# Feed-forward stages of a two-block transformer: gate and up products with the tokens stationary and 512 weight columns moving

## The reference

```python
def rms_norm(x, g):
    xf = x.astype(jnp.float32)
    y = xf * lax.rsqrt(jnp.mean(xf * xf, axis=-1, keepdims=True) + NORM_EPS)
    return (y * g.astype(jnp.float32)).astype(x.dtype)

def swiglu_ffn(h, w_in, w_out):
    gate, up = jnp.split(h @ w_in, 2, axis=-1)
    return (jax.nn.silu(gate) * up) @ w_out

x = x + FFN_RES_WEIGHT * swiglu_ffn(rms_norm(x, ffn1_norm_g[l]), ffn1_w_in[l], ffn1_w_out[l])
```

## Time and profile before

| quantity | value |
|---|---|
| median of 3 runs | 2745.47 us (2745.07 to 2746.79) |
| the profiled execution | 2742.86 us |
| its span, first to last instruction | 2740.9 us |
| mean granted TensorE clock | 0.973 of full speed |
| PE busy | 2630.0 us, 18787 matmul records |
| DVE busy | 1700.7 us |
| ACT busy | 1028.4 us |
| weights cast by ACT in feed-forward steps (L1150) | 132, 1915 ns each |
| low parts by DVE there (L1407) | 132, 2290 ns each |

### The profile page before, as it was taken

The page is one execution under the profiler, slowest core; times in us unless marked ns, Lnnn a source line. Parts: engine busy times, 40 slices in busy tenths (PEclk is TensorE's granted clock), DMA queues, the critical chain, the costliest instruction groups (busy, mean ns, idle before and its releaser), DMA issues. The chain is left out here.

```text
span 2740.9 us, 44687 instructions
## 1 busy us (share of the span) xinstructions
PE 2630.0 (96%) x18787; PEld 2324.0 (85%) x18787; DVE 1700.7 (62%) x2283; ACT 1028.4 (38%) x1275; POOL 99.2 (4%) x179
## 2 busy tenths in 40 slices
PE   8999989999989999989999999999999999989999
PEld 7999888989989999779899954355799899737999
DVE  6887655768768877656678822553455455354555
ACT  4335302444343354204443321643333333264333
POOL 2110000001101100000001000000000000000000
PEclk9999989999999999989999999889999999999999
DMA  8775201647766764004557752100355555210452
GB/s 277 261 260 185 93 1 47 200 140 244 261 216 223 264 224 154 16 1 138 171 174 258 260 193 77 46 1 31 127 183 183 199 184 185 78 62 31 140 183 93
DMA packets 279510, 415.63 MB, mean 152 GB/s; under 512 B 10105, under 2 KB 235721, under 8 KB 277698
## 3 DMA queue, kind: packets, MB, share of 16 engines
q1 hardware_dynamic: 260332, 348.16, 38.5%
q0 software_dynamic: 18128, 64.20, 6.8%
q10 hardware_dynamic: 902, 1.15, 0.1%
HBM read 399.82 MB, written 13.65 MB: 151 GB/s over the span
## 5 line engine op out<-in xcount | busy, mean ns | idle before, releaser
L614 PE MATMUL ps<-h_high,w_high 128*128 128x256 f32 x1984 | 567.9, 286 | 17.5 <-DVE w_low L1407 10.5
L616 PE MATMUL ps<-h_high,w_low 128*128 128x256 f32 x2016 | 572.3, 284 | 0.0
L614 PEld LDWEIGHTS ps<-h_high,w_high 128*128 128x128 f32 x1984 | 382.8, 193 | 20.3 <-DVE w_low L1407 11.4
L616 PEld LDWEIGHTS ps<-h_high,w_low 128*128 128x128 f32 x2016 | 389.0, 193 | 0.0
L1407 DVE TENSOR_TENSOR w_low<-ring,w_high 128x2048 fp32r<-128x2048 f32 x132 | 302.3, 2290 | 138.5 <-ACT w_high L1150 138.2
L615 PE MATMUL ps<-h_low,w_high 128*128 128x256 f32 x1312 | 373.4, 285 | 0.0
L2797 DVE TENSOR_TENSOR w_low<-ring,w_high 128x2048 fp32r<-128x2048 f32 x96 | 220.0, 2292 | 240.6 <-ACT w_high L2581 240.4
L1150 ACT ACTIVATE w_high<-ring 128x2048 fp32r<-128x2048 f32 x132 | 252.3, 1915 | 266.7 <-DMA ring<-in_ffn_w_in 147.9
L2581 ACT ACTIVATE w_high<-ring 128x2048 fp32r<-128x2048 f32 x96 | 183.8, 1916 | 331.2 <-PE ps L2260 304.1
L615 PEld LDWEIGHTS ps<-h_low,w_high 128*128 128x128 f32 x1312 | 254.0, 194 | 0.0
L1428 DVE SCALAR_TENSOR_TENSOR mod_acc<-wmod,cond,mod_acc 128x512 f32<-128x512 f32 x336 | 230.8, 748 | 0.0
(11 more groups left out here) (426 smaller groups left out, 5395.0 us busy)
## 6 DMA issues: line engine op xcount, KB each, us to landing
ring<-in_w_mlp SPq DMA_DIRECT2D x96, 1024.0 KB, 5.5
ring<-in_ffn_w_in SPq DMA_DIRECT2D x88, 1024.0 KB, 8.8
wmod<-in_w_mod POOLq DMA_DIRECT2D x96, 512.0 KB, 6.3
ring<-in_ffn_w_out SPq DMA_DIRECT2D x44, 1024.0 KB, 5.1
ring<-in_w_mix_in SPq DMA_DIRECT2D x26, 1024.0 KB, 5.5
ring<-in_xattn_w_kv SPq DMA_DIRECT2D x16, 1024.0 KB, 5.3
mod_scratch<-mod_acc POOLq DMA_DIRECT2D x24, 512.0 KB, 5.5
ring<-mod_scratch SPq DMA_DIRECT2D x12, 1024.0 KB, 6.8
```

Source lines behind the costliest of these rows:

```text
L614: mm(dst, w_hi, x_hi, start=start, stop=False, **more)
L616: return mm(dst, w_lo, x_hi, start=False, stop=stop, **more)
```

## The change

In all four stages the gate and up products are turned round. 128 tokens of x times the gain (`g_high`, `g_low`) are stationary, and the moving operand is 256 gate columns and 256 up columns of the weights in one access pattern, 512 wide. A step does the first 128 tokens (`half` 0), then the other 128, each into a bank of its own that holds gate and up side by side. For this the two high parts must lie at one stride, so their buffers are laid out in one tensor `span`, two pairs of gate and up, and the down high part has one buffer alone (the storage of `h_high`). The three float32 factors are the same.

The root of the norm is now a number per partition (`root_col`), made by sums on PE with one column; silu takes it as a scale, and the product with up multiplies by it. So the normalised copies for these stages go, and with them `first_apart`, `first_scaled` and two of the three `norm` calls.

The activation now has tokens on partitions. Four PE transposes (`turn`) bring it back, into a PSUM bank of its step; ACT casts the high part from there (`cast`) and DVE subtracts (`act_lower`). `turn(i + 1)` stands in the middle of `down(i)`.

```diff
+            def half_products(b, t, k, last=False):
+                out = ps[4 + 2 * b + t].rearrange("p (r n) -> p r n", r=2)
+                toks, cols, s = slice(t * P, (t + 1) * P), slice(k * BLK, (k + 1) * BLK), tiles.slot(0, b)
+                hi, lo = gate_up_high[b][:, :, cols], w_low[:, s:s + 2, cols]
+                mm(out, g_high[:, k, toks], hi, start=(k == 0), stop=False)
+                mm(out, g_high[:, k, toks], lo, start=False, stop=False)
+                if not last:
+                    return mm(out, g_low[:, k, toks], hi, start=False, stop=(k == KD - 1))
+                for r in range(2):
+                    mm(out[:, r, :], g_low[:, k, toks], hi[:, r, :], start=False, stop=(r == 1)
+                       ).then_inc(w_used[tiles.slot(r, b)].sem, 1)
...
+            def turn(i, b):
+                pe.wait_ge(*tiles.act(i, 2))
+                for t in range(2):
+                    for m in range(2):
+                        at = b * 512 + t * BLK + m * P
+                        last = nc.tensor.transpose(ps[4 + 2 * b][:, m * T + t * P:m * T + (t + 1) * P],
+                                                   act_tok[:, at:at + P], ident)
+                last.then_inc(act_turned.sem, 1)
...
             with pe.Fori(1, FFN_STEPS // 2) as j:
-                gate_up(j * 2 + 1, 1, j * 6 + 2, 2, True)
-                down(j * 2, 0, j * 6 + 4, 1)
-                gate_up(j * 2 + 2, 0, j * 6 + 5, 2, True)
-                down(j * 2 + 1, 1, j * 6 + 7, 1)
+            with pe.Fori(1, FFN_STEPS // 2 - 1) as j:
+                gate_up(1, j * 6 + 2)
+                down(j * 2, 0, j * 6 + 4, lambda: turn(j * 2 + 1, 1))
+                gate_up(0, j * 6 + 5)
+                down(j * 2 + 1, 1, j * 6 + 7, lambda: turn(j * 2 + 2, 0))
...
             with act.Fori(1, FFN_STEPS // 2) as j:
-                silu(j * 2, 0, j, True)
-                w_high_of(0, 1, j, 2, (0, 0, j))
-                w_high_of(1, 1, j, 0, (1, 0, j))
-                w_high_of(2, 0, j, 1, (2, 1, j - 1))
-                silu(j * 2 + 1, 1, j, True)
-                w_high_of(0, 0, j + 1, 2, (0, 1, j))
-                w_high_of(1, 0, j + 1, 0, (1, 1, j))
-                w_high_of(2, 1, j, 1, (2, 0, j))
+            with act.Fori(1, FFN_STEPS // 2 - 1) as j:
+                silu(j * 2, 0, j)
+                w_high_part(tiles, 2, 0, j, DOWN_HIGH, (2, 1, j - 1))
+                cast(j * 2, 0)
+                gate_up(0, j + 1, (1, 0, j))
+                silu(j * 2 + 1, 1, j)
+                w_high_part(tiles, 2, 1, j, DOWN_HIGH, (2, 0, j))
+                cast(j * 2 + 1, 1)
+                gate_up(1, j + 1, (1, 1, j))
...
+            def times_up(i, b, use):
+                for t in range(2):
+                    dve.wait_ge(*tiles.silu(i, t))
+                    if t:
+                        dve.wait_ge(*tiles.used(1, b, use))
+                    at = t * BLK
+                    v.scalar_tensor_tensor(act_tok[:, b * 512 + at:b * 512 + at + BLK], ps[4 + 2 * b + t][:, BLK:2 * BLK],
+                                           root_col[:, t:t + 1], prob[:, b, at:at + BLK], ALU.mult, ALU.mult
+                                           ).then_inc(act_ready.sem, 1)
...
+            def rest(i, b, down_at, chunk, gate_up_at):
+                k = 4 * b
+                modulate(l, f, chunk, range(k, k + 1))
+                w_low_of(2, b, down_at, DOWN_HIGH)
+                act_lower(i, b)
+                modulate(l, f, chunk, range(k + 1, k + 2))
+                if gate_up_at is not None:
+                    w_low_of(0, b, gate_up_at, GATE_UP_HIGHS[b][0])
+                modulate(l, f, chunk, range(k + 2, k + 3))
+                if gate_up_at is not None:
+                    w_low_of(1, b, gate_up_at + 1, GATE_UP_HIGHS[b][1])
+                modulate(l, f, chunk, range(k + 3, k + 4))
```

More of the change, by code:

```diff
@@ L300, in build_first @@
     with ExitStack() as under:
+        span = under.enter_context(nc.sbuf_tensor("span", [P, SPAN], F32R))
+    with ExitStack() as under:
         part = lambda name, shape: under.enter_context(nc.sbuf_tensor(name, shape, F32R))
@@ L619, in ffn, with parts @@
             tiles = FfnTiles(l, f)
-            def parts(r, b, t, buffer):
+            def parts(b, t):
                 pe.wait_ge(*tiles.split(t, w_low_ready))
[L624 to L638, removed]
-                    last.then_inc(w_used[tiles.slot(r, 0)].sem, 1)
+                return [ap.rearrange("p (k n) -> p k n", k=2)
+                        for ap in (w_high[DOWN_HIGH], w_low[:, tiles.slot(2, b), :])]
@@ L675, in down, with tiles_half, gate_up @@
-            def down(i, b, t, buffer):
-                hi, lo = parts(2, b, t, buffer)
+                    for t in range(2):
+                        for k in (2 * p, 2 * p + 1):
+                            last = half_products(0, t, k, t == 1 and k == KD - 1)
+                        if t == 0 and p == KD // 2 - 1:
+                            last.then_inc(*tiles_half())
+            def tiles_half():
+                return half_done.sem, 1
+            def gate_up(b, t, between=None):
+                pe.wait_ge(*tiles.split(t + 1, w_low_ready))
+                for half in range(2):
+                    for k in range(KD):
+                        last = half_products(b, half, k, half == 1 and k == KD - 1)
+                    if half == 0:
+                        last.then_inc(*tiles_half())
+                        if between:
+                            between()
@@ new lines, in ffn @@
+            for r in range(2):
+                w_low_of(r, 1, 2 + r, GATE_UP_HIGHS[1][r])
+            dve.wait_ge(*std_ready.at(l, 6 * f + 2))
+            times_up(0, 0, 0)
+            rest(0, 0, 4, 0, 5)
+            times_up(1, 1, 0)
+            rest(1, 1, 7, 0, 8)
+            with dve.Fori(1, FFN_STEPS // 2 - 1) as j:
+                times_up(j * 2, 0, j)
+                rest(j * 2, 0, j * 6 + 4, j, j * 6 + 5)
+                times_up(j * 2 + 1, 1, j)
+                rest(j * 2 + 1, 1, j * 6 + 7, j, j * 6 + 8)
@@ L1698, in vector_program @@
                  par_ready)
-            norm(l, 0, "ffn1_norm_g")
             if l == 0:
+                for q in range(4):
+                    gained_low(0, 0, q)
                 w_low_part(FfnTiles(0, 0), 1, 0, 1, 1)
```

268 lines of the change are left out of this document (119 added, 149 removed).

## The result

The changed kernel takes 2986.86 us (median of 4 runs, 2973.79 to 2990.12), the kernel before 2745.44 beside it: ratio 1.087 with a 95% interval of 1.084 to 1.090, 241 us slower. The forecast was 2956 with a range of 2885 to 3005, so direction and range held, and the sum is 31 us short.

A forecast was written before the change was run, and what follows sets the result against it. PE, 96% busy, was taken as the bound before, and a loop through loads, casts and DVE after the change. 2742.9 + 174 (stalls) + 43 (clock) - 6 (starts) = 2954, as median 2956 us; range 2885 to 3005.

The forecast's parts named there:

- The loop: Feed-forward steps: end of one down product leads through loads, casts, DVE and transposes to the next; 22.1 us.
- PE's stall: PE stands 5.5 us in front of the transposes of every step in the loop, making steps 4.8 us longer.
- the price of the wide matmul: Gate and up products: a 512-column matmul taken at 0.216 us, giving 10.4 us per step instead of 11.5.
- The upper bound of 0.240: Gate and up products: a 512-column matmul costs at most twice 0.120 us, by which the products gain nothing.
- rival 2: Feed-forward steps: the loop doesn't close, PE stays the bound, 2730 us, faster; chance 0.07.
- its other branch, 2779: No loop and PE the bound, with 512-column matmuls at 0.240 us: a step 17.7 us, time 2779; chance 0.02.
- The clock: PE's clock falls after each stall, through transposes and half down product: 1.2 us a step, +43 us in all.
- The upper bound of 1.4: Most that low clock behind a stall could cost per step: 11.5 x 0.12 = 1.4 us.
- The last down product: End of each stage: weights share the single down buffer, so cast, low part and act_low make PE wait 5.1 us.
- The starts: Stage starts: gate and up no longer wait for a normalised copy; -6 us taken (-15 to +5).
- rival 3: More waits: a modulation store that shows, or low clock beyond the loop's part; some 3010 us; chance 0.05.
- Rival 1: Loop closes, but clock stays 2.4 GHz (2913 us) or burst lands earlier (2906), both 2863; chance 0.26 together.

## Why the prediction was right, and where it was short

**The loop: right, through a slightly other member.** The end of down i-1 leads over the next loads, casts and DVE's product to the transposes in down i. Either side, moved alone, takes off more than half of the loss; both together take off 225 of 250 us. The forecast path from issue to transposes was 12.0 + 1.95 + 2.21 + 1.33 + 0.95 = 18.4; measured are 8.17 + 1.95 + 2.21 + 1.33 + 2.21 + 1.32 + 0.93 = 18.1. In this step and 25 others of the 32 the up weights landed earlier (cast at 11.1, not 12.0), but DVE came to them only at 123.45: the gate low part and two modulation operations were still ahead. From the gate cast on the chain is DVE's, and an earlier up load alone gains nothing. In the other six steps the path is the forecast's, through the up cast. That the sum fits by either path is in part luck: by the forecast's own rows the gate path (8.2 + 1.95 + 2.21 + 1.33 = 13.7) and the up path (12.0 + 1.95 = 13.95) reach the up low part 0.3 us apart, and the prediction weighed only the second.

**PE's stall: 4.0 to 4.5 us, not 5.5**, in the 26 steady steps (5.3 to 7.0 in the six with late up weights). Of the difference 0.3 us are the shorter path and 0.7 PE's work, which was mis-sized; the rest I didn't break down. With 0.231 it is 47 x 0.231 + 0.24 + 0.44 + 5.76 = 17.3 us, and not 16.6. The step of the forecast that failed is the price of the wide matmul, 0.216: it held that the excess over the column count is a weight load that 512 columns hide. At 2.4 GHz 256 columns take 0.120 (288 cycles, 32 in excess), and 512 take 0.231 (554, 42 in excess): it isn't hidden. The upper bound of 0.240 was the nearer end. What that excess is was not found. In the total this is hidden in the stall, as the prediction said; it matters only once the loop is gone, where rival 2, which keeps the single down buffer, gave 2730. The measured 2750 with all orders moved and one down buffer lies between that and its other branch, 2779.

The Trainium skill, "TensorE: Matmul & The Clock Gate", section "Back-to-back issue gap", gives 215.8 ns for 512 columns by a formula that it calls the isolated gap, and says that this formula gives too much for a stream, where it has 131 ns. The rows here show 231 ns in a stream of this type, with pieces or without, which is more than either; the measurement decides.

**The clock: there, and dearer.** Forecast 1.2 us a step. From the transposes to SP's issue are 3.64 us at full clock; measured are 5.19 (127.91 to 133.10) and 5.95 (151.14 to 157.09), so 1.55 and 2.3, and keeping PE busy gave back about 2. In all 32 steps this stretch takes at least 5.05 us. The upper bound of 1.4 was too low: it was read over the 3.3 us behind one stall, and here the windows show a low clock over 5.3 and 6.1 us.

The Trainium skill, the same page, section "HAM oscillation — how this bites in real kernels", has such a wait throttle the engine anew each time. The windows of 0.68 and 0.58 after stalls of some 4 us agree.

**Steps.** Forecast 22.1 + 1.2 = 23.3, measured 23.0 to 24.1 in the steady steps, and on average 6.75 us above before over the 32 steps of the four stages, where 4.8 + 1.2 = 6.0 were forecast. That is 24 us more than forecast, half of it in the six steps with late up weights. At the landmark the forecast's terms make 174 + 43 - 6 = 211 us and 250.4 were measured; the other 15 lie in the starts and ends of the stages. Behind the landmark 4.2 us came back, which no term foresaw.

**The last down product: 4 x 5.1, exactly**, and the run with one buffer shows it as a cause by itself.

**The starts: a loss.** I took -6 us. From the first down issue of a stage to its third it takes 7.2, 2.3, 1.6 and 0.7 us longer than before, 11.8 in all, which includes the wait of step 1's transposes (2.1 us in each stage, where 2 were forecast). The first product of the first stage now waits for both low parts and begins at 25.61 after 7.97 us of idle, where it began at 20.22. The third down issue, 52.04 before, comes at 59.24.

**The modulation store (rival 3)** was rightly held hidden in the changed kernel: DVE waits 2.82 us at 130.67, when PE already has what it needs. With another order of SP it costs 2.3 us every second step, and some 1.4 more of low clock behind it. The time that the prediction gives for this rival doesn't follow from its terms: 9 x 1.4 + 5 x 1 per stage are 70 us in four stages, so some 3026 and not 3010.

**Rival 1** fell: the clock didn't stay, and the earlier landing of the up weights bought nothing. Nor does the modulation load tell early landings from late ones: it goes out in every burst, some 6.4 us after the down issue.

## What to carry to other kernels

When an operation of an in-order queue comes to stand behind a wait for a transfer, and the transfer's issue waits for what that operation feeds, there is a loop. Add it up once round and compare with the bound engine's work per step: the greater one is the step. Here it had to be opened on both sides (SP's order and those of ACT and DVE): opened on one side alone it closed again through the next transfer, or through DVE's own order. And price a wider matmul at the bound at which it gains nothing, until a row shows it.

## What the runs showed of the hardware

- A reduced float32 matmul starts every 0.120 us with 256 columns (0.118 in pairs on the same weights) and every 0.231 us with 512, alike for two pieces of 256 and for 512 neighbouring columns, all at the full granted clock. What the excess over the column count is stays open.
- Stalls of 4 us and more brought the clock down in the steps of the changed kernel: windows of 0.68 and 0.58, and in all 32 steps 5.05 to 6.30 us from the transposes to the issue, where it is 3.64 at full clock. With dummy matmuls in the stalls the same stretch took no more than 3.7 us in 29 of 32 steps (mean clock 0.972). The length of a stall alone doesn't tell: 1.84 us in the earlier trace rows left the clock at 1.00, and in the kernel with ACT's and DVE's orders moved it is 0.67 behind a stall of 1.85 us (at 112.10) and 1.00 behind one of 2.66 us (at 783.45).
- In the same untouched code, over 340 us of time, one execution was granted 1.00 and another 0.90: 30 us from one to the other. A landmark behind the changed code tells 10 us where the total doesn't.
- A gate load behind the same down load was cast 8.2 us after the issue in the changed kernel. With ACT's and DVE's orders moved it was cast 8.8 to 10.8 us after it in the 16 bursts without a modulation store near the issue, and 11.0 to 12.5 in the 16 with one. That the store is the cause wasn't tried by itself.
